# MLP products of a two-layer encoder in float32: seven block products for eight, in separate up and down stages, with the activations in DRAM

## What is computed

```
mix = concatenate([oa, ob, oc, od], axis=-1) @ w_out[l]
x = x + rms_norm(mix, norm_mix_post[l])
h = rms_norm(x, norm_mlp_pre[l])
f = square(relu(h @ w_up[l])) @ w_down[l]      # 1024x1024 by 1024x4096, then by 4096x1024
x = x + rms_norm(f, norm_mlp_post[l])
```

## Time and profile before

| | |
|---|---|
| runs | 3195.16 us, median of 3 (3194.68 to 3196.55) |
| profiled execution | span 3193.2 us, first to last instruction; mean clock 0.954 |
| TensorE | 2920.7 us busy, 91% of the span |
| VectorE, ScalarE, POOL | 1519.4, 1218.9, 701.6 us |
| DMA | 219.75 MB, mean 69 GB/s |

### The profile page before, as it was taken

One profiled execution on the slowest core, in us unless ns is written; L12 is line 12 of the kernel. 1 busy time (PEld: TensorE's weight loads), 2 busy tenths in 40 slices (PEclk: granted clock), 3 DMA queues, 4 the chain that ended last, 5 costly groups with the idle time before them and its releaser, 6 DMA issues. The chain is left out here.

```text
span 3193.2 us, 37806 instructions
## 1 busy us (share of the span) xinstructions
PE 2920.7 (91%) x14640; PEld 2429.2 (76%) x14640; DVE 1519.4 (48%) x2342; ACT 1218.9 (38%) x2134; POOL 701.6 (22%) x359
## 2 busy tenths in 40 slices
PE   4997998887989999999969979988878999999997
PEld 3986887665778888888748869867756888888886
DVE  3613866975632222322564157679654322222226
ACT  3412766864422211111333147668643112222114
POOL 1222001850022222222021210038201222222220
PEclk8998998998999999999979989989988999999998
DMA  6242032441221111111333310344222111111104
GB/s 191 64 137 71 1 80 41 72 126 53 66 86 53 53 53 47 41 44 49 93 92 91 126 40 1 80 77 82 80 73 79 53 53 53 53 53 53 53 20 119
DMA packets 208821, 219.75 MB, mean 69 GB/s; under 512 B 75255, under 2 KB 168187, under 8 KB 208381
## 3 DMA queue, kind: packets, MB, share of 16 engines
q1 hardware_dynamic: 208624, 217.24, 24.8%
q10 hardware_dynamic: 12, 0.02, 0.0%
HBM read 168.99 MB, written 48.59 MB: 68 GB/s over the span
## 5 line engine op out<-in xcount | busy, mean ns | idle before, releaser
L204 PE MATMUL u_ps<-h_hi,up_w_h 128*128 128x512 f32 x1024 | 401.2, 392 | 7.5 <-PEq L148 7.1
L205 PE MATMUL u_ps<-h_lo,up_w_h 128*128 128x512 f32 x1024 | 400.4, 391 | 0.0
L1900 ACT ACTIVATE wd_h<-wd_raw 128x1024 fp32r<-128x1024 f32 x64 | 66.1, 1056 | 680.2 <-PE d_ps L1859 568.0
L1859 PE MATMUL d_ps<-wd_h,up_h 128*128 128x512 f32 x1024 | 318.0, 392 | 5.0 <-DVE m_acc L1955 3.3
L1961 DVE TENSOR_TENSOR m_square<-m_relu 128x1024 f32<-128x1024 f32 x64 | 99.3, 1552 | 467.7 <-ACT m_relu L1904 467.6
L1955 DVE TENSOR_TENSOR m_acc<-m_acc,d_ps 128x512 f32<-128x512 f32 x224 | 143.4, 684 | 371.0 <-PE d_ps L1859 357.9
L208 PE MATMUL u_ps<-h_hi,up_w_l 128*128 128x512 f32 x1024 | 317.0, 391 | 0.0
L1859 PE MATMUL d_ps<-wd_l,up_h 128*128 128x512 f32 x1024 | 315.6, 389 | 0.0
L1859 PE MATMUL d_ps<-wd_h,up_l 128*128 128x512 f32 x1024 | 315.4, 389 | 0.0
L1826 POOL TENSOR_TENSOR wd_l<-wd_raw,wd_h 128x1024 fp32r<-128x1024 f32 x64 | 153.0, 2401 | 611.6 <-ACT wd_h L1900 610.9
L1820 POOL TENSOR_TENSOR up_w_l<-up_w_raw,up_w_h 128x1024 fp32r<-128x1024 f32 x62 | 171.9, 2773 | 450.0 <-ACT up_w_h L1894 450.0
(11 more groups left out here) (259 smaller groups left out, 6204.7 us busy)
## 6 DMA issues: line engine op xcount, KB each, us to landing
up_w_raw<-in_w_up SPq DMA_DIRECT2D x64, 512.0 KB, 4.3
wd_raw<-in_w_down SPq DMA_DIRECT2D x64, 512.0 KB, 4.2
w_raw<-in_w_in SPq DMA_DIRECT2D x16, 512.0 KB, 4.2
cd_v<-v_out SPq DMA_DIRECT2D x16, 512.0 KB, 3.3
cd_qk<-p_h SPq DMA_DIRECT2D x16, 512.0 KB, 2.6
cd_qk<-p_l SPq DMA_DIRECT2D x16, 512.0 KB, 3.8
c_q_s<-cd_qk SPq DMA_DIRECT2D x16, 512.0 KB, 8.4
c_k_s<-cd_qk SPq DMA_DIRECT2D x16, 512.0 KB, 16.6
```

The source lines that it names most:

```text
L204: nc.tensor.matmul(o, w_hi, x_hi[:, tok], start=first, stop=False)
L205: nc.tensor.matmul(o, w_hi, x_lo[:, tok], start=False, stop=False)
L1859: last = nc.tensor.matmul(d_ps[:, (d0 + n) % 4, :], lhs[:, k, tok], rhs[:, k, n * HALF:(n + 1) * HALF], start=(k == 0 and rhs is d_h and l ...
```

## The change

The MLP stage becomes two. Products are made by 2x2 blocks in the form with seven block products and sums on both sides (the blocks are halves: of the tokens, of the inner dimension, and of the columns).

- **POOL and SP in attention a and b** make the four sums of blocks of w_down that the down stage needs: 17 steps in a, 15 in b. A step loads 2 x 256 KB, makes four sums of 128x256 on POOL and stores 2 x 256 KB to down_sums, in the half of mix not yet written.
- **Out stage**: the turned tokens are kept as float32, h_f, with their block sums in h_d, which VectorE makes for tiles 4 to 7 in four pieces each. The first up weights (1 MB) are loaded, not split.
- **Up stage**, 16 pairs of 128-feature blocks. First ScalarE and VectorE split seven token blocks (hc_h, hc_lf, hc_ld). Per pair VectorE makes four weight sums (s1 to s4), seven low parts and the sums, relu and square of the results; ScalarE makes seven high parts, two copies (p1, p5) and a relu. Block weights lie in rings of eight. TensorE makes 7 products of 12 matmuls. Seven blocks per pair (the activations and their sums) go to act_blocks, 1.8 MB per pair.
- **Down stage**, seven products of eight blocks n (56). Block n loads 512 KB of act_blocks and 512 KB of w_down or down_sums into one of three buffers; ScalarE rounds 2048 elements per partition, VectorE subtracts, TensorE makes 24 matmuls. Sums of products are evacuated between them; the near tiles' norms run beside blocks 44 to 50, the last four blocks are done tile by tile. x has two buffers.

The core of the diff (the new stages' code; the old ones stand above; indentation shortened):

```diff
+for j in range(len(steps)):
+    if j + 1 < len(steps):
+        load(j + 1)
+    store(j)
...
+def make_sums(pool, steps):
+    for j in range(len(steps)):
+        raw, dst = sum_blocks(j)
+        pool.wait_ge(S[f"sum_landed{j % 2}"], 32 * (j // 2 + 1))
+        if j >= 2:
+            pool.wait_ge(S[f"sums_stored{j % 2}"], 32 * (j // 2))
+        nc.gpsimd.tensor_tensor(dst[:, 0, 0], raw[:, 0, 1], raw[:, 0, 0], ALU.subtract) \
+            .then_inc(S["sum_step"], 1)
+        nc.gpsimd.tensor_tensor(dst[:, 1, 0], raw[:, 1, 1], raw[:, 0, 1], ALU.subtract)
+        pool.wait_ge(S["sum_step"], 2 * j + 1)
+        nc.gpsimd.tensor_tensor(dst[:, 0, 1], raw[:, 1, 1], dst[:, 0, 0], ALU.subtract) \
+            .then_inc(S["sum_step"], 1)
+        pool.wait_ge(S["sum_step"], 2 * j + 2)
+        nc.gpsimd.tensor_tensor(dst[:, 1, 1], raw[:, 1, 0], dst[:, 0, 1], ALU.subtract) \
+            .then_inc(S["sums_done"], 1)
+steps_a, steps_b = range(0, SUMS_IN_A), range(SUMS_IN_A, 2 * NPAIR)
...
+after(nc.vector.tensor_tensor(h_d[:, LOW, near], turned[:, LOW, :], h_f[:, LOW, near], ALU.subtract))
+after(nc.vector.tensor_tensor(h_d[:, HIGH, near], turned[:, HIGH, :], h_d[:, LOW, near],
+                              ALU.subtract))
+nc.vector.tensor_tensor(h_d[:, LOW, far], h_f[:, HIGH, far], turned[:, LOW, :], ALU.subtract)
+nc.vector.tensor_tensor(h_d[:, HIGH, far], h_f[:, HIGH, near], h_d[:, HIGH, near],
...
+tok_blocks = ((h_f, hc_lf, LOW, NEAR), (h_d, hc_ld, LOW, NEAR), (h_d, hc_ld, LOW, FAR),
+              (h_f, hc_lf, HIGH, NEAR), (h_d, hc_ld, HIGH, NEAR), (h_f, hc_lf, HIGH, FAR),
+              (h_d, hc_ld, HIGH, FAR))
...
+    raw = up_raw[:, m % 2]
+    return (raw[:, LOW, FIRST], s1[:, :, :], s3[:, :, :], raw[:, HIGH, FIRST], s2[:, :, :], s4[:, :, :], raw[:, HIGH, SECOND])[j]
+bank_of = (0, 2, 3, 0, 1, 2, 3)
+opens = (True, True, True, False, True, False, False)
...
+def store(m):
+    sp.wait_ge(S["staged"], m + 1)
+    sp.dma_start(act_blocks[:, m].rearrange("s p n -> p s n"), stage[:, m % 2]) \
+        .then_inc(S[f"u_stored{m % 2}"], 16)
...
+for m in range(NPAIR):
+    for j in range(7):
+        x = 7 * m + j
+        pe.wait_ge(S["w_lo"], x + 1)
+        if m == 0:
+            pe.wait_ge(S["hc_lo"], j + 1)
+        if j == 0 and m >= 2:
+            pe.wait_ge(S["posts_done"], m - 1)
+        if j == 3:
+            pe.wait_ge(S["p1_copied"], m + 1)
+        if j == 5:
+            pe.wait_ge(S["p5_copied"], m + 1)
+        if j == 6:
+            pe.wait_ge(S["p7_added"], m + 1)
+        dst = bank(m, bank_of[j])
+        for k in range(KT // 2):
+            pairs = ((w_h, hc_h[:, j, k, :]), (w_h, tok_low(j)[:, k, :]), (w_l, hc_h[:, j, k, :]))
+            for i, (wt, tok) in enumerate(pairs):
+                last = nc.tensor.matmul(dst, wt[:, x % RING, k, :], tok,
+                                        start=(opens[j] and k == 0 and i == 0),
+                                        stop=(k == KT // 2 - 1 and i == 2),
+                                        skip_group_check=not opens[j])
...
+for j in range(7):
+    tok_high(j)
+    weight_high(j)
+    if j == 3:
+        copy_product(0, 0, p1, "p1_copied")
+    if j == 4:
+        copy_product(0, 1, p5, "p5_copied")
...
+def weight_low(x):
+    if x < 7 * NPAIR:
+        dve.wait_ge(S["w_hi"], x + 1)
+        nc.vector.tensor_tensor(w_l[:, x % RING], weight_block(x), w_h[:, x % RING], ALU.subtract) \
+            .then_inc(S["w_lo"], 1)
+def posts(m, j):
+    u = stage[:, m % 2]
+    dve.wait_ge(S["gemm_done"], 7 * m + j + 1)
+    if j == 2:
+        dve.wait_ge(S["p5_copied"], m + 1)
+        nc.vector.tensor_tensor(t57, p5, bank(m, 3), ALU.add).then_inc(S["p7_added"], 1)
+    if j == 3:
+        dve.wait_ge(S["relu11"], m + 1)
+        nc.vector.tensor_tensor(u[:, 0], u[:, 0], u[:, 0], ALU.mult)
+    if j == 4:
+        after(nc.vector.tensor_tensor(u2, p1, bank(m, 1), ALU.add))
+    if j == 5:
+        after(nc.vector.tensor_tensor(u[:, 3], u2, bank(m, 2), ALU.add))
+        square(u[:, 3])
+def late_posts(m):
+    u = stage[:, m % 2]
+    nc.vector.tensor_tensor(u[:, 1], u2, bank(m, 3), ALU.add).then_inc(S["posts_done"], 1)
+    dve.wait_ge(S["p7_added"], m + 1)
+    after(nc.vector.tensor_tensor(u[:, 2], u2, t57, ALU.add))
+    dve.wait_ge(S["posts_done"], m + 1)
+    after(square(u[:, 1:3]))
+    after(nc.vector.tensor_tensor(u[:, 4], u[:, 3], u[:, 2], ALU.add))
+    nc.vector.tensor_tensor(u[:, 3], u[:, 0], u[:, 3], ALU.subtract)
+    after(nc.vector.tensor_tensor(u[:, 5], u[:, 4], u[:, 0], ALU.subtract))
+    nc.vector.tensor_tensor(u[:, 6], u[:, 1], u[:, 5], ALU.subtract).then_inc(S["staged"], 1)
...
+weight_sums(0)
+for j in range(7):
+    tok_lo(j)
+    weight_low(j)
+weight_low(7)
+weight_sums(1)
+for m in range(NPAIR):
+    for j in range(7):
+        posts(m, j)
+        weight_low(7 * m + j + RING)
+    if m + 2 < NPAIR:
+        weight_sums(m + 2)
...
+with ExitStack() as c, nc.Block() as block:
+    NG = NPAIR // 2
+    N_ALL = 7 * NG
+    TAIL = N_ALL - 4
...
+act_of = (0, 4, 1, 6, 5, 3, 2)
+opens = (True, True, False, False, True, True, False)
+bank0 = (0, 4, 0, 4, 0, 4, 4)
...
+def load(n):
...
+def part(n, q, i):
+    pi, g = n // NG, n % NG
+    for lhs, rhs in ((g_h, g_h), (g_h, g_l), (g_l, g_h)):
+        first = g == 0 and q == 0 and lhs is g_h and rhs is g_h
+        last = nc.tensor.matmul(d_ps[:, bank0[pi] + i, :], lhs[:, n % 4, 0, q, i * P:(i + 1) * P],
+                                rhs[:, n % 4, 1, q, :], start=(opens[pi] and first),
+                                stop=(g == NG - 1 and q == 1 and lhs is g_l),
+                                skip_group_check=not opens[pi])
...
+for n in range(TAIL):
+    pi, g = n // NG, n % NG
+    pe.wait_ge(S["d_lo"], n + 1)
+    if g == 0 and 2 <= pi < 5:
+        pe.wait_ge(S["evac_done"], pi - 1)
+    if n == 5 * NG:
+        pe.wait_ge(S["taken"], 1)
+    for q in range(2):
+        for i in range(HT):
+            if n == 6 * NG and q == 0:
+                pe.wait_ge(S["final_done"], i + 1)
+            last = part(n, q, i)
+    last.then_inc(S["gemm_done"], 1)
+    s = n - (5 * NG + 7)
+    if 0 <= s < HT:
+        turn(s)
+for i in range(HT):
+    for n in range(TAIL, N_ALL):
+        if i == 0:
+            pe.wait_ge(S["d_lo"], n + 1)
+        for q in range(2):
+            last = part(n, q, i)
+    last.then_inc(S["tile_done"], 1)
...
+def high(n):
+    if n % 3 == 2 or n >= 3:
+        act.wait_ge(S[f"raw_landed{n % 3}"], landed(n))
+    if n >= 4:
+        act.wait_ge(S["gemm_done"], n - 3)
+    nc.scalar.activation(g_h[:, n % 4], dn_raw[:, n % 3], ACT.Copy).then_inc(S["d_hi"], 1)
...
+for n in range(N_ALL):
+    high(n)
+    if n == NG + 3:
+        evacuate(0, c_far[:, :, NEAR])
+    if n == 2 * NG + 3:
+        evacuate(1, c_far[:, :, FAR])
+    if n == 3 * NG + 3:
+        evacuate(2, c_near[:, :, NEAR])
+    if near_turned(n) >= 0:
+        tok_high(near_turned(n))
+    k = n - (5 * NG + 4)
+    if 0 <= k < 8:
+        norm_step(0, k)
+for k in range(8):
+    if k >= 4:
+        tok_high(HT + k - 4)
+    norm_step(HT, k)
...
+for n in range(N_ALL):
+    if n == 6 * NG + 3:
+        dve.wait_ge(S["gemm_done"], 6 * NG)
+        for i in range(HT):
+            nc.vector.tensor_tensor(c_far[:, i, FAR], c_far[:, i, FAR], d_ps[:, 4 + i, :], ALU.add) \
+                .then_inc(S["final_done"], 1)
+        dve.wait_ge(S["final_done"], HT)
+        nc.vector.tensor_tensor(c_far[:, :, FAR], c_far[:, :, FAR], c_far[:, :, NEAR], ALU.add) \
+            .then_inc(S["final_done"], 1)
+    low(n)
+    if n == 4 * NG + 3:
+        dve.wait_ge(S["gemm_done"], 4 * NG)
+        dve.wait_ge(S["evac_done"], 3)
+        nc.vector.tensor_tensor(c_near[:, :, FAR], c_far[:, :, NEAR], d_ps[:, 4:8, :], ALU.add) \
+            .then_inc(S["taken"], 1)
+    if n == 5 * NG + 3:
+        dve.wait_ge(S["gemm_done"], 5 * NG)
+        dve.wait_ge(S["taken"], 1)
+        nc.vector.tensor_tensor(c_near[:, :, FAR], c_near[:, :, FAR], d_ps[:, 0:4, :], ALU.add) \
+            .then_inc(S["acc_done"], 1)
+        nc.vector.tensor_tensor(c_far[:, :, NEAR], c_far[:, :, NEAR], d_ps[:, 0:4, :], ALU.add) \
+            .then_inc(S["taken"], 1)
+        dve.wait_ge(S["taken"], 2)
+        dve.wait_ge(S["gain_landed"], 32)
+    k = n - (5 * NG + 4)
+    if 0 <= k - 1 < HT:
+        step = post_norm(k - 1)
...
+        step = pre_norm(k - 2)
+    if near_turned(n) >= 0:
+        tok_low(near_turned(n))
+dve.wait_ge(S["final_done"], HT + 1)
+for k in range(8):
+    if k < HT:
```

512 lines of the change are left out of this document (282 added, 230 removed).

## The result

The changed kernel takes **3099.09 us** (median of 4 runs, 3096.73 to 3099.99) against 3194.92 us in the same comparison: ratio 0.9701, 95% interval 0.9687 to 0.9715, about 96 us less. The forecast was 3112.2 us, a gain of 83.

The account below looks back on a forecast made before the run. TensorE was taken to bound the MLP. Per layer, 87.5 us saved less 46.0 of new cost (11.9 + 14.9 + 47.3 + 2 - 30.1) gains 41.5, both layers 83.0: 3112.2 us, range 3093 to 3148.

Parts of the forecast that it names:

- What goes: MLP: seven block products instead of eight remove 384 matmuls, exactly one chunk of D_FF, -87.5 us per layer.
- TensorE alone bounds the MLP: MLP of the kernel before: TensorE busy all of the time mid-window, a chunk 87.48 us, 0.228 us per matmul.
- Up stage, start: Before the first matmul VectorE's sums and low parts take 5.7 us; with low clock and t57 wait 11.9 together.
- The wait for t57: Up stage, first pair: TensorE's last product waits for a sum standing behind VectorE's low parts, 3.5 us.
- Up stage, steady: VectorE needs 16.8 of TensorE's 19.1 us per pair, so its work is hidden and costs nothing.
- Between up and down: Last pair's sums 5.7 us, store of 1.8 MB 8.0, stage change 1.2: 14.9 us.
- Down stage: Start 4.4 us, low clock 2.7 twice, wait for c_far sum at block 48 11.0, transposes 4.0, tail 22.5: 47.3.
- Other places: POOL's weight sums in attention a and b cost nothing; the out stage gets +2 us (0 to 4) per layer.
- (1): Rival, up stage: VectorE's 23 instructions per pair set the pace, 30 us per pair, 3460 us; 4%.
- (2): Rival, down stage: the loads set the pace, 8.4 us per block, 3440 us; 6%.
- (3): Rival, attention a and b: POOL's sums outlast them at 6.5 us per step, 3178 us; 7%.
- (4): Rival: more hand-over stalls than counted, such as at blocks 44 to 49, 5 to 15 us per layer, 3120 to 3142; 13%.

Follow-up runs that it names:

- experiment 1: Changed kernel with one of the down stage's seven block products done twice, so eight as in the old form: 3185.39 us, ratio 0.9970.
- the runs of 6: Single edits of the changed kernel: c_far sums earlier 3087.42 us, t57 earlier 3091.85, last store not waited for 3086.87, residuals of tiles 6 and 7 in dn_raw 3086.07.
- experiment 7: Changed kernel with VectorE's low part for tiles 0 to 3 and TensorE's wait for it put back in the out stage: 3105.90 us, ratio 0.9725.
- 8: Changed kernel with all four edits of the runs of 6 together, and tiles 1 to 3 read out one block earlier: 3047.74 us, ratio 0.9541.
- t57_early: Changed kernel with the first pair's t57 moved on VectorE behind the sixth low part, ahead of the last token block: 3091.85 us, ratio 0.9672.

## Why the prediction was right

**What goes** was right, and experiment 1 shows it directly for the down stage: a block product is worth its matmuls. The term was 3 us per layer too small. I had priced a matmul at 87.48/384 = 0.228. In the changed kernel 380 matmuls lie between 999.73 and 1085.86, 0.2267 each, and the old chunk is 384 of these and 0.44 us. That rest was no work of TensorE's but a wait for VectorE, in each chunk where the down products of the third token tile begin (TensorE, its weight load, VectorE):

```profile
2606.55 0.61 PE L1859 MATMUL d_ps<-wd_h,up_l 128*128 128x512 f32 x2
2607.29 0.73 PE L1859 MATMUL d_ps<-wd_h,up_h 128*128 128x512 f32 x2
...
2607.28 0.30 PEld L1859 LDWEIGHTS d_ps<-wd_h,up_h 128*128 128x128 f32 x2 [0.54 <-DVE m_acc L1955]
...
2605.95 2.55 DVE L1955 TENSOR_TENSOR m_acc<-m_acc,d_ps 128x512 f32<-128x512 f32 x4 [3.92 <-PE d_ps L1859]
```

The third tile writes the PSUM of the first (acc_done). The first tile's product is complete only after 42 matmuls of the chunk's down products, six before the third tile starts, and the two sums of m_acc that read it end a little too late. So "TensorE alone bounds the MLP" was not quite true of the kernel before, and the new stages, which have no such wait, are free of it in all their matmuls.

**Up stage, start**: 5.6 for 5.7. The wait for t57 is 2.7 where I took 3.5, but the clock falls with it, which the text says of every longer rest and the term leaves out: seven more matmuls 0.43 apart, 1.4 us. **Up stage, steady**: hidden, as forecast, with more room than I gave it. **Between up and down**: the store was the mis-sized term, about 6.6 us for 8.0. I went by the nearest size among the rows; the estimate of 6.2 from the Trainium skill, DMA: Bandwidth & Descriptors, section Anatomy of one DMA, was nearer, although the page gives its formula for transfers issued from GpSimd and this store is issued from SyncE. **Down stage**: block 48 at 10.89 for 11.0, the tail at 23.05 for 22.5, the rest 1 us below. That is the clock: I had charged 2.7 us after each of two rests, and it was 1.6 at the stage's start (seven matmuls in 3.15 us instead of 1.59) and 2.4 after block 48. That they were caused as described is shown for the sum, t57, the store and x by the runs of 6, each of which removed one.

**Other places** was the step with the wrong sign. For the out stage I counted VectorE's instructions and not what waited for them. The 2 us that I counted are there: 1.0 us before the last transposes (7.48 us of idle time for 6.46) and 1.1 between them and the stage's last instruction. But TensorE's transposes of tile 2 had stood behind h_lo, and experiment 7 puts 3.9 us per layer on that, clock included. For POOL's sums "nothing" stands: no cost in a or b shows beyond the scatter between traces. The remaining 1.8 us per layer lie mostly in the first stages, up to attention a, and are within what these stages differ by from trace to trace.

The rivals: (1) and (2) had 4% and 6% and were far off. VectorE has over 3 us per pair to spare, and loads twice as large stay hidden, so (2) was given too much. (3) is real as a mechanism, but needs five or six steps more in a than its 17 (4.3 us each, and 26.7 us are left there, 4.6 of them for the last store and the stage change). (4) did not show, but a stall of its kind was there: the one at block 48 hid the wait of 4.59 us that experiment 6 uncovered. The error of 13 us is in the main matmul price (6), out stage (8) and store (3), less what other stages lost by scatter (4); the other terms nearly cancel.

## What to carry to other kernels

With TensorE busy nine tenths of the time, the work taken from it was worth its price here; what decided the rest were the hand-overs that the new form adds, and each could be worked out from single durations by writing down what stands behind what on each engine's list, SP's among them, and who waits for an instruction that is taken away. A stall that is removed may have been lending time to another engine: move what that engine owes in the same edit, as in 8. And test whether an engine or a queue is near its limit by giving it more work, not by its busy share.

## What I had not expected of the hardware

- Sixteen DMA engines that show a share of 0.60 at 192 GB/s still took 380 GB/s without delaying TensorE; only the time of each transfer doubled (3.9 to 7.4 us for 512 KB).
- VectorE with a backlog runs at 98.7% busy with instructions of 0.68 us, with no visible cost between them.
- POOL beside VectorE makes an SBUF-only instruction of VectorE 2.4 times as long (0.69 to 1.67), enough to make VectorE busier (217 us for 197) after 30% of its instructions were taken away.
- The same rest did not always cost the same: after 17.8 us between the stages TensorE's first 7 matmuls were slow (0.43 us apart) in one trace and 13 in another (changed kernel and t57_early, second layer), and 1.45 us of rest cost no clock where 3.80 did.
